# Interleaving the first mixer's two head groups, and norms, transposes and first product tiles by row tile and feature block, in a two-block float32 program

## The reference

```python
# first block
h = rms_norm(x, g_mix_norm); z = h @ w_in          # q_m k_m v_m o_m gates c_q c_kv k_pe
y_a = mlstm_group(...)   # 4 heads, both directions, chunks of 128, C and n carried over chunks
y_b = mla_group(...)     # 4 heads, softmax(q k^T * scale) v over all 512 keys
x = x + concat([y_a, y_b]) @ w_out
h = rms_norm(x, g_ffn_norm)
x = x + square(relu(h @ w_ff1)) @ w_ff2
# second block
h = rmsnorm(x, norm_mix_g); proj = h @ w_in_2
ret_out = silu(rg) * rmsnorm(retention(rq, rk, rv))           # 4 heads, chunks of 128
diff_out = rmsnorm(softmax(s0) @ v - lam * softmax(s1) @ v)   # 4 heads, causal, ALiBi
x = x + concat([ret_out, diff_out]) @ w_out_2
x = x + peer(rmsnorm(x, norm_ffn_g), wq, subkeys, u, v)       # top 16 of 16384 experts, 8 heads
return rmsnorm(x, final_norm_g)
```

## Time and profile before

| | us |
|---|---|
| three runs | 2561.06, 2564.78, 2567.64 |
| median | 2564.78 |
| the profiled execution | 2563.88 |
| its span in the trace | 2562.1 |

### The profile page before, as it was taken

One profiled execution on the slowest core, in us unless ns is written; L12 is line 12 of the kernel. 1 busy time (PEld: TensorE's weight loads), 2 busy tenths in 40 slices (PEclk: granted clock), 3 DMA queues, 4 the chain that ended last, 5 costly groups with the idle time before them and its releaser, 6 DMA issues.

```text
span 2562.1 us, 29145 instructions
## 1 busy us (share of the span) xinstructions
PE 2404.5 (94%) x11589; PEld 1209.4 (47%) x11797; DVE 1329.6 (52%) x2379; ACT 805.9 (31%) x880; POOL 847.1 (33%) x221
## 2 busy tenths in 40 slices
PE   7987889999989888889999999999999999999998
PEld 3456445444444454444466544444444444444443
DVE  2654526454532542689999555555555552222223
ACT  3221324333332333211189532222222232323222
POOL 0000215555553144531000253333333333424231
PEclk9985899999999999999999999999999999999999
DMA  5010035988863105763467986666666657666531
GB/s 202 33 66 1 1 148 164 246 246 244 247 191 105 66 34 169 215 176 119 160 273 303 345 241 188 184 182 185 184 186 180 182 176 201 170 174 180 138 91 41
DMA packets 401649, 424.98 MB, mean 166 GB/s; under 512 B 275578, under 2 KB 342270, under 8 KB 388740
## 3 DMA queue, kind: packets, MB, share of 16 engines
q1 hardware_dynamic: 395204, 411.93, 53.2%
q10 hardware_dynamic: 6336, 11.54, 1.2%
HBM read 283.97 MB, written 72.35 MB: 139 GB/s over the span
## 4 chain that ended last, share of the span: by engine, by line
PE 74%; DVE 17%; ACT 4%; DMA 2%; issue 2%; POOL 1%; DVEq 0%; SPq 0%; POOLq 0%; ACTq 0%
PE ps L1490 43%; PE ps L1765 14%; DVE arena L2428 5%; DVE arena L2435 4%; PE ps L1803 2%; DMA gate_matrix<-split 2%; PE ps L1303 2%; ACT split L1224 2%; PE ps L1588 1%; ACT arena L1210 1%; PE ps L1301 1%; PE ps L1276 1%; PE ps L1781 1%; PE ps L1432 1%; PE ps L1782 1%
## 5 line engine op out<-in xcount | busy, mean ns | idle before, releaser
L1490 PE MATMUL ps<-split,arena 128*128 128x512 bf16 x4232 | 936.6, 380 | 22.8 <-DVE x_sb L2450 9.0
L1490 PEld LDWEIGHTS ps<-split,arena 128*128 128x128 bf16 x4320 | 421.2, 98 | 534.1 <-DVE x_sb L2450 14.4
L852 POOL TENSOR_TENSOR split<-ring,split 128x4096 bf16<-128x4096 f32 x32 | 259.3, 8103 | 892.1 <-ACT split L1224 892.1
L1765 PE MATMUL ps<-arena 128*128 128x512 bf16 x1881 | 415.4, 379 | 2.1
L2450 DVE TENSOR_TENSOR x_sb<-ps,x_sb 128x512 f32<-128x512 f32 x256 | 173.8, 689 | 323.2 <-PE ps L1490 323.2
L759 POOL TENSOR_TENSOR split<-ring,split 128x4096 bf16<-128x4096 f32 x27 | 215.2, 7970 | 293.3 <-ACT split L1001 266.5
L1490 PE MATMUL ps<-arena,split 128*128 128x512 bf16 x1314 | 293.8, 381 | 13.1 <-DVE arena L2156 6.6
L2428 DVE TENSOR_TENSOR arena<-arena 128x512 f32<-128x512 f32 x128 | 179.7, 1404 | 238.4 <-ACT arena L1217 142.1
L1765 PEld LDWEIGHTS ps<-arena 128*128 128x128 bf16 x1920 | 187.9, 98 | 226.5
L1490 PEld LDWEIGHTS ps<-arena,split 128*128 128x128 bf16 x1344 | 142.7, 107 | 158.4 <-issue 9.8
L2435 DVE TENSOR_TENSOR arena<-arena 128x512 bf16<-128x512 f32 x128 | 157.2, 1228 | 67.4 <-ACT arena L1210 33.7
(11 more groups left out here) (300 smaller groups left out, 2457.6 us busy)
## 6 DMA issues: line engine op xcount, KB each, us to landing
ring<-in_peer_v SPq DMA_DIRECT2D x32, 2048.0 KB, 7.7
ring<-in_peer_u SPq DMA_DIRECT2D x20, 2048.0 KB, 8.3
ring<-in_w_ff SPq DMA_DIRECT2D x16, 2048.0 KB, 8.3
gate_matrix<-split SPq DMA_DIRECT2D x16, 2048.0 KB, 8.2
arena<-gate_matrix SPq DMA_DIRECT2D x32, 1024.0 KB, 8.4
arena<-in_peer_u SPq DMA_DIRECT2D x48, 512.0 KB, 4.7
turned_table<-u_split SPq DMA_DIRECT2D x48, 512.0 KB, 5.4
ring<-turned_table SPq DMA_DIRECT2D x12, 2048.0 KB, 9.5
```

The source lines that it names most:

```text
L852: pool.tensor_tensor(split[:, s2, 1, :], ring[:, slot, :], split[:, s2, 0, :], ALU.subtract).then_inc(w_lo, 1)
L1490: mm = pe.matmul(dst, a(k), b(k), start=n == 0, stop=n == len(terms) - 1)
L1765: mm = pe.matmul(up_bank(j), a, b, start=n == 0, stop=n == len(terms) - 1)
```

## The change

Every line number of the changed kernel below is its own. In words:

1. **Attention between the parts of the mLSTM heads.** `attend(i)` holds score(i), turn(i-1), value(i-2). In head h PE runs scores, link 4h, update, link 4h+1, values, inter, links 4h+2 and 4h+3; two turn/value remainders follow after the heads. Banks: the mLSTM keeps 0, 2 to 5 and the attention gets one bank each for score (1), turn (6) and value (7), so score(i) waits for exp(i-1). POOL makes the inverse rms head by head, and splits the first out weight in quarters between them; ACT's sigmoid comes first, and `head_rows` of head h-1 runs in head h.
2. **Norms by row tile.** POOL's inverse rms becomes four one-column calls for ffn, mix2 and peer; `norm_row(t-1)` follows the last add of row tile t; `turn_features` transposes blocks 0 to 3 row tile by row tile, as each arrives. mix2 gets banks 0, 1, 2, 3, 0, 1, 6, 7.
3. **First product tile by feature block.** Instead of all 8 low parts first, `three_pass` waits for `turned_hi` k before high block k, and for `turned_lo` k in the pass that reads it.
4. **Differential attention.** The exponential is written to the PSUM bank of the score, and L2292, L2294 read it there. A score waits for `dif_probs` instead of `dif_max`; a step is ten matmuls, score(i+1), turn(i-1), four matmuls, value(i-2), the rest. DVE's y2 copy comes after the maxima.
5. **PEER.** `up` tiles 0 and 1 no longer wait for the last `key_tops`; tiles 2 and 3 wait for the 15th and 16th.

```diff
-        TURN_BANKS = (0, 1, 4, 5)
+        def turn_bank(stage, k):
+
+            return (0, 1, 2, 3, 0, 1, 6, 7)[k] if stage == "mix2" else (0, 1, 4, 5)[k % 4]
...
+            def mlstm_rms(h):
+                inverse_rms(NT, DV, 3 * NT + NT * (h + 1), h * NT)
+
+            mlstm_rms(0)
+            mlstm_rms(1)
+            pool.wait_ge(w_hi, 1)
+            for q in range(4):
+                cols = slice(q * 1024, (q + 1) * 1024)
+                first_low = pool.tensor_tensor(split[:, 0, 1, cols], ring[:, 1, cols], split[:, 0, 0, cols], ALU.subtract)
+            first_low.then_inc(w_lo, 1)
+            mlstm_rms(2)
+            mlstm_rms(3)
 
             def split_low(s, s4):
...
 
-            inverse_rms(NT, D, 36)
...
                 for d in range(2):
                     act.activation(num[:, d, :, :], bank(4 + d).rearrange("p (c v) -> p c v", c=NC), ACT.Copy).then_inc(num_out, 1)
+                attend_exp(4 * h + 2)
+                attend_exp(4 * h + 3)
 
                 act.wait_ge(head_out, h + 1)
...
-                act.activation(att[:, i % 2, :], bank(2 + i % 2), ACT.Exp, bias=row_nmax[:, i:i + 1], scale=A_DH ** -0.5,
...
-                    act.activation(split[:, s, 0, :], ring[:, 1 + s, :], ACT.Copy).then_inc(w_hi, 1)
-
             def turned_high(stage, gain, hi=xT_hi):
...
-                    act.activation(dif[:, i % 2, m, 0:n_keys], dif[:, i % 2, m, 0:n_keys], ACT.Exp, bias=row_nmax[:, 2 * i + m:2 * i + m + 1],
+                    act.activation(bank(4 * (i % 2) + m)[:, 0:n_keys], dif[:, i % 2, m, 0:n_keys], ACT.Exp, bias=row_nmax[:, 2 * i + m:2 * i + m + 1],
                                    accum_out=row_sum[:, 2 * i + m:2 * i + m + 1]).then_inc(dif_exp, 1)
...
-            pe.wait_ge(mm_out, 16)
-            pe.wait_ge(nope_out, 2 * NT)
-            pe.wait_ge(rope_out, NT)
-            pe.wait_ge(v_put, 2 * NT)
-            for h in range(H):
+            def head_update(h):
+
                 at = (h % 2) * DQK
-                mlstm_scores(h)
-
                 pe.wait_ge(kdec_done, h + 1)
+                if h >= 1:
...
-                if h < H - 1:
-                    pe.wait_ge(head_read, h + 1)
-
-
-            pe.wait_ge(num_out, 2 * H)
-            pe.wait_ge(head_out, H)
...
+            def attend_score(i):
+
+                h, q = divmod(i, NT)
+                if i >= 1:
+                    pe.wait_ge(att_exp, i)
+                at = slice(h % 2 * A_ROPE, (h % 2 + 1) * A_ROPE)
+                pe.matmul(bank(1), nopeT[:, h, q * P:(q + 1) * P], nopeT[:, H + h, :], start=True, stop=False)
+                pe.matmul(bank(1), ropeT[at, h // 2, q * P:(q + 1) * P], ropeT[at, 2 + h // 2, :],
+                          start=False, stop=True).then_inc(att_scores, 1)
+
+            def attend_turn(n):
+
+                pe.wait_ge(att_exp, n + 1)
+                if n >= 1:
+                    pe.wait_ge(att_out, n)
+                for i in range(NT):
+                    mm = pe.transpose(bank(6)[:, i * P:(i + 1) * P], att[:, n % 2, i * P:(i + 1) * P], ident)
+                mm.then_inc(att_turned, 1)
+
...
+            def attend(i):
+
+                attend_score(i)
+                if i >= 1:
+                    attend_turn(i - 1)
                 if i >= 2:
...
+                    attend_value(i - 2)
...
+            for h in range(H):
+                if h >= 1:
+                    pe.wait_ge(head_read, h)
+                mlstm_scores(h)
+                attend(4 * h)
+                head_update(h)
+                attend(4 * h + 1)
+                head_values(h)
+                head_inter(h)
+                attend(4 * h + 2)
+                attend(4 * h + 3)
+            attend_turn(H * NT - 1)
+            attend_value(H * NT - 2)
+            attend_value(H * NT - 1)
+
...
-            def three_pass(dst, hi, lo, w_hi_, w_lo_, steps):
+                for t in range(NT):
+                    if rows_done is not None:
+                        pe.wait_ge(xn_done, rows_done + t + 1)
+                    for k in range(4):
+                        mm = pe.transpose(bank(turn_bank(stage, k))[:, t * P:(t + 1) * P], src_k[:, t, :, k], ident)
+                        if t == NT - 1:
+                            mm.then_inc(turned, 1)
+                for k in range(4, KD):
+                    pe.wait_ge(turned_lo, TURN_LO[stage] + k - 3)
+                    turn(k, turn_bank(stage, k), lambda t: src_k[:, t, :, k])
+
+            def three_pass(dst, hi, lo, w_hi_, w_lo_, steps, turning=None, low_pass=None):
 
                 terms = [(a, b, k) for a, b in ((hi, w_hi_), (hi, w_lo_), (lo, w_hi_)) for k in range(steps)]
                 for n, (a, b, k) in enumerate(terms):
+                    if turning is not None and n < steps:
+                        pe.wait_ge(turned_hi, TURN[turning] + k + 1)
+                    if turning is not None and n // steps == low_pass:
+                        pe.wait_ge(turned_lo, TURN_LO[turning] + k + 1)
                     mm = pe.matmul(dst, a(k), b(k), start=n == 0, stop=n == len(terms) - 1)
...
-                                        lambda k: hi[:, k, :], lambda k: lo[:, k, :], KD)
...
-                linear_chunk(S_OUT + c, MM["out"] + 4 * c, False)
-
-
...
                 if i >= 2:
-                    pe.wait_ge(dif_max, 2 * (i - 1))
+                    pe.wait_ge(dif_probs, i - 1)
...
                 at = dif_share(i)
+                in2_matmuls(at, at + 10)
                 if i + 1 < H * NT:
                     dif_score(i + 1)
-                in2_matmuls(at, at + 6)
                 if i >= 1:
                     dif_turn(i - 1)
-                in2_matmuls(at + 6, at + 12)
+                in2_matmuls(at + 10, at + 14)
                 if i >= 2:
                     dif_value(i - 2)
-                in2_matmuls(at + 12, dif_share(i + 1))
+                in2_matmuls(at + 14, dif_share(i + 1))
 
             def ret_score(i):
...
                 mm.then_inc(gate_mm, 1)
 
-            pe.wait_ge(key_tops, 2 * P_HEADS)
             for m in range(SELECTED):
+                if m in (2, 3):
+                    pe.wait_ge(key_tops, 2 * P_HEADS - 3 + m)
...
+            def attend(i):
+
+                if i < H * NT:
+                    dve.wait_ge(att_scores, i + 1)
+                    own.did(dve.tensor_reduce(row_max[:, i:i + 1], bank(1), AX.X, ALU.max))
+                    own.wait()
+                    dve.tensor_scalar(row_nmax[:, i:i + 1], row_max[:, i:i + 1], -(A_DH ** -0.5), None, ALU.mult).then_inc(att_max, 1)
+                if 1 <= i <= H * NT:
+                    n = i - 1
+                    dve.wait_ge(att_turned, n + 1)
+                    if n >= 2:
+                        dve.wait_ge(att_pv, n - 1)
+                    dve.tensor_copy(attT[:, n % 2, :], bank(6)).then_inc(att_out, 1)
...
+                attend(4 * h)
...
+
+                dve.wait_ge(num_done, h + 1)
+                own.did(dve.tensor_copy(den, bank(0)[:, 0:8].rearrange("p (a b) -> p a b", a=2)))
                 dve.wait_ge(num_out, 2 * h + 2)
-                dve.wait_ge(num_done, h + 1)
-                own.did(dve.tensor_copy(den, bank(1)[:, 0:8].rearrange("p (a b) -> p a b", a=2)))
                 dve.wait_ge(inter_done, h + 1)
                 for d in range(2):
...
                             own.did(step)
...
+                attend(4 * h + 3)
+                if h == 0:
...
                     dst = x_sb[:, t, c * CW:(c + 1) * CW]
                     dve.tensor_tensor(dst, bank(2 + (done_before + n) % 2), dst, ALU.add).then_inc(mm_out, 1)
-
-            def norm_rows(rstd_count):
-                dve.wait_ge(rstd_done, rstd_count)
-                for t in range(NT):
-                    dve.tensor_scalar(xn[:, t, :], x_sb[:, t, :], rstd[:, t:t + 1], None, ALU.mult).then_inc(xn_done, 1)
+                    if n >= 5:
+                        norm_row(rstd_count, t - 1)
+                norm_row(rstd_count, NT - 1)
+
+            def norm_row(rstd_count, t):
+                dve.wait_ge(rstd_done, rstd_count + t)
+                dve.tensor_scalar(xn[:, t, :], x_sb[:, t, :], rstd[:, t:t + 1], None, ALU.mult).then_inc(xn_done, 1)
 
             turned_low("out", G_Y1)
-            add_linear(MM["out"])
-            norm_rows(4)
+            add_linear(MM["out"], 7)
             turned_low("ffn", G_FFN)
...
             for i in range(H * NT + 3):
-                if i >= 3:
-                    n = i - 3
-                    h, q = divmod(n, NT)
-                    dve.wait_ge(dif_pv, n + 1)
...
+                    own.did(dve.tensor_scalar(dif[:, n % 2, 0, 0:n_keys], bank(4 * (n % 2))[:, 0:n_keys], row_inv[:, 2 * n:2 * n + 1], None, ALU.mult))
                     own.wait()
-                    dve.scalar_tensor_tensor(dif[:, n % 2, 0, 0:n_keys], dif[:, n % 2, 1, 0:n_keys], row_inv[:, 2 * n + 1:2 * n + 2],
```

(1 more changed line is left out.)

214 lines of the change are left out of this document (102 added, 112 removed).

## The result

| | before | changed |
|---|---|---|
| median of 4 runs, us | 2565.47 | 2474.48 |
| lowest, highest | 2561.06, 2567.64 | 2467.71, 2482.43 |
| ratio | | 0.9649, 95% interval 0.9614 to 0.9683 |
| span of the profiled execution | 2562.1 | 2476.2 |
| its mean granted clock | 0.965 | 0.987 |

The change takes 91.0 us off the median, 3.5%. The prediction was 2480, the range 2462 to 2518. What first meets the eye is the spread: 14.7 us between four runs of the changed kernel, against 6.6 of the one before.

What follows compares the result with a forecast made beforehand. PE, with 74% of the chain, was taken as the bound, losing time to waits and a low clock. Savings of 46.9 + 1.4 + 6.0 + 3.8 + 18 + 0.4 + 8.5 + 0.5 = 85.5 us gave 2480 us, range 2462 to 2518.

Steps and rivals of the forecast that it cites:

- Merged stage: mLSTM heads with attention links between their parts: 115.8 us against 162.7, so 46.9 us less.
- single score bank: In the merged heads, each score waits for the previous exponential: a new wait of 0.4 us a head.
- about 8 us into the stretch of links: In head 0 PE's clock falls, then returns about 8 us into the gapless links; head 0 takes 36.1 us.
- Rival B: In merged heads, update, values and inter parts pull the clock down again: 26 us lost, 2505 us; chance 0.20.
- rival C: All four merged heads stay at the lower clock, broken by transposes: 72 us lost, 2552 us; chance 0.10.
- Turns: Shorter gaps before products: out 1.4, feed-forward 6.0, mix2 3.8, out2 0.4, peer 8.5 us saved.
- norm rows: Before the feed-forward block, rows 0 to 2 normed under the products leave one row's norm, saving 2.06 us.
- Differential attention: New step order and exponential in PSUM in the differential attention: 18 us saved, bounds 8 and 24.
- order term: Differential attention: removing 19.0 us of turn waits and some 5 us of low clock, at most 24 us.
- PSUM term: Differential attention: DVE reading PSUM instead of SBUF costs at most 6 us, all taken off the gain.
- Part 5: PEER gates: starting up tiles earlier fills PE while DVE sorts, saving 0.5 us, bounds 0 to 3.
- Rival D: Merged links hide nothing and run serially at the lower clock: stage 248 us, whole 2612 us; chance 0.03.

Runs made afterwards that it cites:

- links_last: The changed kernel with all 16 attention links behind the four mLSTM heads again, single banks kept: 2531.44 us, ratio to before 0.9875.
- tile_waits_all: The changed kernel with the first product tile waiting for all eight low parts again, in all five turns: 2482.64 us in one run.
- links_first: The changed kernel with another order in head 0 alone, link 0 before the scores and links 1 and 2 before the update: 2478.87 us, ratio 0.9664.
- wide_once: The kernel before with eight extra unused float32 matmuls of 512 columns once, between mLSTM heads 0 and 1: 2565.43 us in one run.
- norms_last: The changed kernel with DVE's four norm rows behind all adds again in ffn, mix2 and peer: 2474.82 us in one run.
- dif_sbuf_exp: The changed kernel with the differential attention's exponential back in SBUF and the score waiting for dif_max, new order kept: 2488.29 us in one run.

## Why the prediction came out right, step by step

The sum of 85.5 us is close to the 85.9 us between the two spans, and most of its large steps are right in kind. But two of them came out by luck in part: head 0, and the differential attention, in which two errors cancel.

- **Merged stage**: 46.9 us forecast, 47.3 measured (115.8 against 115.4 us). Head 0 was to take 36.1 us and took 36.15; heads 1 to 3 24.1 each, measured 24.3 and 24.6 for two of them; the tail 6.2, and from 251.69 to 282.02 less a head of 24.3 it is 6.0. The 0.4 us a head for the single score bank were 0.3. The 1.2 us that I gave to ACT's copy in head 2 hardly show: that head took 0.3 us more than head 1. (18.6 / 1.87 is 9.9 and not 10.1, an error of 0.2 us a head.) links_last shows that the order makes the gain. But the agreement in head 0 is luck: the same code took 22.9 and 27.1 us in other executions. My "about 8 us into the stretch of links" is one outcome out of at least three, and belonged in the sum as a range of -13 us.
- **The clock**: I took the row in which 8.16 us without a gap were followed by the full clock, and set the 9.86 us of values that were not beside it. The profile after agrees with my reading by shape, and does not prove it: PE had no gap from 166.63 on, the clock fell at 168.5 and was back at 199.2, some 6.5 us into links 2 and 3. But tile_waits_all ran the same head parts at 1.00, and in links_first, with three links early in head 0, the clock was down until 192.6 all the same. Rival B (the parts of a head pull the clock down again) does not happen from head 1 on, and rival C neither, though transposes stand in every link. The rule of the Trainium skill ("TensorE: Matmul & The Clock Gate", Part 4: PE-mode transpose) of which I made rival C does not show here: the merged heads keep 1.00 with four turns in each. In the kernel before something like B does happen: in wide_once the clock fell again within 14 us, though behind a wait of 3.33 us, which the merged heads do not have.
- **Turns**: forecast 1.4, 6.0, 3.8, 0.4 and 8.5, together 20.1. Measured from the table: 2.7 (1.7 of it a dip of the clock that did not occur), 5.2, 3.0 (6.0 less the 3.0 in the feed-forward block), -0.5 and 9.1, together 19.5. The sum is right and the working half wrong. I gave 2.06 us a turn to the norm rows that run under the products; norms_last shows 0 for that place, and a loss of 4 at mix2, of which the stall of 2.26 us (I had put it at 2.0) is behind L2237 and GpSimd's L777, as the earlier trace rows had let me expect. I gave part 3 too little; tile_waits_all has 12 to 13 us for it.
- **Differential attention**: 18 forecast, 19.7 measured, by two errors that cancel. The order term was 24 us (19.0 of waits and 5 of clock), and the order gives 10.5 to 12.9 without PSUM: turns still waited 9.6 us in dif_sbuf_exp. The PSUM term has the wrong sign: I took up to 6 us off for it, since an L2165 read from PSUM is slower than an SBUF read, and it gave 6.8 us on top of the new order. With both, turns and scores wait 6.2 us in place of 19.0 (I had said under 5), and the clock is 1.00 in the window. I had the 5.52 us wait in the earlier trace rows before me and did not ask why one step waits for so long. The quiet price was about right for the first of the two operations (0.41 to 0.61 us) and too high for the second (0.62 in both); what the sum lacked is that beside GpSimd's work they take up to 2.00 and 2.35 us from SBUF. The mean of 4.3 us of DVE a step was nearly enough.
- **Part 5**: 0.5 forecast, 1.0 measured up to the gates. This is no more than the stretch varies between kernels that are the same in it: 240.5 us in the changed kernel and norms_last, 241.9 in dif_sbuf_exp and links_first, 241.4 before.
- **Rival D**, the slower one, did not occur: PE is 99% busy in a merged head.

## What to carry to other kernels

Where two chains of small steps share no data, put the links of one into the waits of the other, and work out the cost of the result at both levels of the clock: here the clock was worth 24.6 us and the waits 22.7, with head 0 at its slowest. Before the gain of a small edit is believed, compare executions in which the clock did the same everywhere else: 13 us of chance in head 0 hid what the last kernels won or lost. A stretch of work that stands idle ahead of a stage is not slack until it is known what the moved work had been covering behind it. And a placement that hides an operation pays only if that operation was late in the first place; ask first what stands idle while it runs.

## What the hardware showed that I had not expected

- In the changed kernel's profile PE ran without a gap from 168.5 to 199.2 at half rate, and kept the full rate through the same kinds of parts in heads 1 to 3. Gaps alone do not tell it: the clock also fell at 154.8, for 3.4 us, when PE had run without a gap since 139.65.
- The same instructions at the same place took 22.9, 27.1 or 36.1 us, by the clock alone. With five 384-column float32 matmuls (3.4 us) ahead of them the spread of five runs was 2.6 us, and 13.1 without.
- Beside GpSimd's work DVE took 0.61 us for 384 columns from PSUM, and 2.00 for the same operation from SBUF, which takes 0.41 when GpSimd is quiet.
